# A hybrid backbone layer with hierarchical experts: router by token halves, four places for projection weights, reordered first unit

## The reference, cut to what matters

```
out_x = (sigmoid(ga) * (ya' @ w_proj_a) + sigmoid(gb) * (yb' @ w_proj_b)) @ w_out
x     = x + mx[2] * out_x
h     = rmsnorm(x, norm2_g) * (1 + mx[4]) + mx[3]
p_grp = softmax(h @ w_rg + b_rg)            # 4 groups, the best one is taken
e_sel = (h @ w_re + b_re) of that group     # 8 experts in it, the best two are taken
cw    = pg * softmax(e_sel)[top 2] / their sum
y     = sum over the 32 experts of cw[:, e] * ((silu(h @ w1[e]) * (h @ w3[e])) @ w2[e])
out   = rmsnorm(x + mx[5] * y, final_g)
```

## Time and profile before

| | us |
|---|---|
| median of 3 runs | 1008.64 (1008.11 to 1009.26) |
| the profiled execution's own time | 1011.78 |
| its span | 1010.0 |
| TensorE busy in the span | 870.7 (86%) |
| VectorE busy | 375.9 (37%) |
| ScalarE busy | 315.1 (31%) |
| moved by DMA | 284.4 MB, 282 GB/s on average |

### The profile page before, as it was taken

One profiled execution on the slowest core, in us unless ns is written; L12 is line 12 of the kernel. 1 busy time (PEld: TensorE's weight loads), 2 busy tenths in 40 slices (PEclk: granted clock), 3 DMA queues, 4 the chain that ended last, 5 costly groups with the idle time before them and its releaser, 6 DMA issues.

```text
span 1010.0 us, 13145 instructions
## 1 busy us (share of the span) xinstructions
PE 870.7 (86%) x4774; PEld 538.4 (53%) x4774; DVE 375.9 (37%) x882; ACT 315.1 (31%) x576; POOL 65.0 (6%) x109
## 2 busy tenths in 40 slices
PE   2999999999999999999998999496555746799796
PEld 1578686868686868688857433222121211343331
DVE  2357575848484848482124624100001000001101
ACT  5373737373746464640003301101010010110211
POOL 1020201111111111120000000000000000000000
PEclk9999999999999999999997999887787877899898
DMA  9956363636363635308699699999999999999993
GB/s 366 321 135 188 94 188 93 187 93 187 93 186 94 180 101 166 83 7 285 215 430 363 249 427 419 430 427 426 429 428 427 428 430 427 427 426 430 426 421 129
DMA packets 125313, 284.37 MB, mean 282 GB/s; under 512 B 6432, under 2 KB 100832, under 8 KB 111456
## 3 DMA queue, kind: packets, MB, share of 16 engines
q1 hardware_dynamic: 124656, 283.30, 74.6%
q10 hardware_dynamic: 624, 0.62, 0.2%
HBM read 282.86 MB, written 1.05 MB: 281 GB/s over the span
## 4 chain that ended last, share of the span: by engine, by line
PE 67%; DMA 25%; issue 3%; DVE 2%; ACT 1%; SPq 1%; POOL 1%; ACTq 0%; DVEq 0%; POOLq 0%
PE bank L549 37%; DMA arena<-in_w 24%; PE bank L838 11%; PE bank L847 4%; PE bank L770 3%; PE bank L857 2%; PE bank L827 2%; DMA arena<-in_c_ctx 1%; PE bank L582 1%; PE bank L637 1%; PE bank L867 1%; PE bank L654 1%; PE bank L663 1%; PE bank L618 1%; PE bank L617 1%
## 5 line engine op out<-in xcount | busy, mean ns | idle before, releaser
L549 PE MATMUL bank<-arena 128*128 128x256 f32 (+3 forms) x1792 | 401.7, 381 | 2.1 <-DVE arena L1240 1.5
L549 PEld LDWEIGHTS bank<-arena 128*128 128x128 f32 x1792 | 299.2, 191 | 86.3 <-issue 56.7
L838 PE MATMUL bank<-arena 128*32 128x512 f32 (+1 forms) x1024 | 159.2, 670 | 69.5 <-DMA arena<-in_w 69.5
L838 PEld LDWEIGHTS bank<-arena 128*32 128x32 f32 (+1 forms) x1024 | 43.9, 128 | 182.7 <-issue 110.8
L847 PE MATMUL bank<-arena 128*32 128x512 f32 (+1 forms) x512 | 80.2, 673 | 28.3 <-DMA arena<-in_w 28.3
L1564 DVE TENSOR_TENSOR arena<-arena,bank 128x512 f32<-128x512 f32 x10 | 10.3, 1030 | 235.3 <-PE bank L838 235.3
L1129 ACT ACTIVATE arena<-bank 128x512 f32<-128x512 f32 x10 | 6.0, 597 | 205.5 <-PE bank L838 205.5
L1571 DVE TENSOR_TENSOR arena<-bank,arena 128x512 f32<-128x512 f32 x20 | 13.8, 692 | 144.9 <-PE bank L847 144.9
L847 PEld LDWEIGHTS bank<-arena 128*32 128x32 f32 (+1 forms) x512 | 21.9, 129 | 79.3 <-issue 48.5
L1133 ACT ACTIVATE arena<-bank 128x256 f32<-128x256 f32 x10 | 3.8, 383 | 138.4 <-PE bank L892 138.4
L827 PE MATMUL bank<-arena 128*128 128x128 f32 x352 | 43.3, 284 | 1.7 <-DVE arena L1544 1.7
(11 more groups left out here) (304 smaller groups left out, 889.5 us busy)
## 6 DMA issues: line engine op xcount, KB each, us to landing
arena<-in_w SPq DMA_DIRECT2D x92, 2048.0 KB, 27.1
arena<-in_w_in SPq DMA_DIRECT2D x72, 512.0 KB, 7.0
arena<-in_w_mod SPq DMA_DIRECT2D x9, 2048.0 KB, 8.1
arena<-in_w SPq DMA_DIRECT2D x8, 1024.0 KB, 22.4
arena<-in_w_mod SPq DMA_DIRECT2D x1, 4096.0 KB, 17.1
arena<-in_w_proj_a SPq DMA_DIRECT2D x8, 512.0 KB, 3.8
arena<-in_w_proj_b SPq DMA_DIRECT2D x8, 512.0 KB, 5.1
arena<-in_w_out SPq DMA_DIRECT2D x2, 2048.0 KB, 9.4
```

The costliest lines, as they stand in the source:

```text
L549: i = mm(dst, w(k), rhs(k), start=k == 0, stop=k == KT - 1)
L838: i = mm(acc[w * b:w * b + w, :], xg[:, k, w * b:w * b + w], wtile(kind, b, u)[:, k, :], start=k == 0, stop=k == KT - 1)
```

## The change

It has these parts.

1. *Projection weights:* `wp` has four places instead of two; blocks 2 and 3 are asked for as soon as the last head's `og`/`ga` product is done. Then SyncE's order is: both halves of w_out, loads 0 and 1 of the experts, blocks 4 and 5, load 2, blocks 6 and 7, load 3, x and final_g, and the other loads from 4 on. Load 4 waits for block 5, load 5 for block 7. RING begins at other places so that this fits. TensorE's loop over blocks is unrolled.
2. *Modulation rows:* diagonals and `gate_rows` go, and so do `spread`, `turned`, `octet` and the matmuls of L808. TensorE turns modB once (`turn_mod`), ScalarE writes the 32 rows of 128 to a buffer in HBM and reads back gate1 and gate2, spread to all partitions, and `mod_pk`, by four DMAs on its own queue.
3. *Router by halves:* the shift term is summed on VectorE first and needs one matmul. TensorE's order is mixed: output part (1,1) is cut in pieces of 2, 4 and 2 of its eight steps, between them the logits of token half 0 and transposes. VectorE does norm and `route(t)` for half 0 while TensorE ends part (1,1), then for half 1. ScalarE makes root and xn half by half.
4. *First gather:* by token half too, with `hot` made straight from the ranks, `idle_work` matmuls whose result nobody reads between its parts, and the copies to xg shared by ScalarE and VectorE.
5. *Unit 0:* its down projection stands before the next gather; `gated(0)` stands before the four sums of the tables rk, ck; loads 10 and 11 (w2 of unit 1, in the places of unit 0's w1) come in two halves, the first when half of the w1 product is done (`m1_half`).

The core of the diff, lines of waits and views left out:

```diff
-RING = tuple(SLOT * i for i in (1, 2, 3, 4, 5, 6, 0)) + (A_T, 7 * SLOT, A_HT)
+RING = tuple(SLOT * i for i in (2, 3, 4, 5, 0, 1, 6)) + (A_T, 7 * SLOT, A_HT)
...
-        wp = [[at(2048 * b + 1024 * j, KT, P) for j in range(2)] for b in range(2)]
+        wp = [[at(2048 * b + 1024 * j, KT, P) for j in range(2)] for b in range(4)]
...
+                if n in (4, 5):
+                    sp.wait_ge(S("proj_mm1"), n - 1)
                 if n == 7:
                     sp.wait_ge(S("wo_mm"), 4)
                 if n == 8:
-                    sp.wait_ge(S("rt_mm"), 1)
+                    sp.wait_ge(S("rt_mm"), 3)
...
+                if n == 10:
+                    sp.wait_ge(S("m1_half"), 1)
+                    for i in range(2):
+                        sp.dma_start(wslot(k, i, at_u)[:, 0:2 * D], src[k][experts[i]][:, 0:2 * D]).then_inc(S("in_w2_1"), 16)
...
+            sp.wait_ge(S("ff_mm"), this(HEADS - 1))
+            proj_loads(0)
+            proj_loads(1)
+            sp.wait_ge(S("og_mm"), this(HEADS - 1))
+            proj_loads(2)
+            proj_loads(3)
+            sp.wait_ge(S("yb_out"), this(HEADS - 1))
+            sp.wait_ge(S("ya_out"), this(HEADS - 1))
+            for i in range(2):
+                sp.dma_start(wo[:, 4 * i:4 * i + 4, :], wo_v[:, 4 * i:4 * i + 4, :]).then_inc(S("wo_in"), 16)
+            sp.wait_ge(S("gb_mm"), this(HEADS - 1))
+            fetch(0)
+            fetch(1)
+            proj_loads(4)
+            proj_loads(5)
+            fetch(2)
+            proj_loads(6)
+            proj_loads(7)
+            fetch(3)
...
-                if first:
-                    gate_rows(b)
+                if first and b == 0:
+                    turn_mod()
+            def turn_mod():
+
+                pe.wait_ge(S("mod_rows"), 1)
+                pe.wait_ge(S("orms_out"), this(HEADS - 1))
+                pe.wait_ge(S("on_out"), this(HEADS - 1))
+                pe.transpose(bank[6][0:4 * KT, 0:P], modB[:], ident[:]).then_inc(S("mod_rows"), 1)
...
-            down_k(bank[2][:, 0:NG + NE], lambda k: ones[:, 0:P], lambda k: w_sh[:, k, :]).then_inc(S("gate_mm"), 1)
+            mm(bank[2][:, 0:NG + NE], ones[:, 0:P], w_sum, start=True, stop=True).then_inc(S("rt_mm"), 1)
             w_out_half(1, 0)
-            turn_x1(0)
-            w_out_half(1, 1)
+            turn_x1(0, 0)
+            turn_x1(0, 1)
+            w_out_half(1, 1, 0, 2)
             pe.wait_ge(S("rt_prep"), 2)
             pe.wait_ge(S("x1T_out"), 2)
-            logits(0)
-            turn_x1(1)
+            logits(0, 0, KT)
+            w_out_half(1, 1, 2, 6)
+            turn_x1(1, 0)
+            w_out_half(1, 1, 6, KT)
+
+            sel = rt[:, 5]
+            pe.wait_ge(S("sel_out"), 1)
+            mm(bank[7][:, 0:NE], before[:], sel[:, 0, :], start=True, stop=True).then_inc(S("rank_mm"), 1)
+            mm(bank[5][:, 0:NE], ones[:, 0:P], sel[:, 0, :], start=True, stop=False)
+            mm(bank[6][:, 0:NE], ones[:, 0:P], sel[:, 0, :], start=True, stop=False)
             pe.wait_ge(S("x1T_out"), 3)
+            logits(1, 0, 2)
+            turn_x1(1, 1)
+            logits(1, 2, 4)
             pe.wait_ge(S("x1T_out2"), 1)
+            logits(1, 4, KT)
...
+            pe.wait_ge(S("hot_first"), 1)
+            pe.wait_ge(S("xn_out"), 1)
+            gather_first(0, 0)
+            gather_first(0, 1)
+            idle_work(4)
+            pe.wait_ge(S("sel_out"), 2)
+            mm(bank[5][:, 0:NE], before[:], sel[:, 1, :], start=False, stop=True).then_inc(S("rank_mm"), 1)
+            mm(bank[6][:, 0:NE], ones[:, 0:P], sel[:, 1, :], start=False, stop=True).then_inc(S("rank_mm"), 1)
+            idle_work(1)
...
-                gather(0)
-                pe.wait_ge(S("gtc"), this(q))
-                gather(1)
+                if u != 0:
+                    gather(0)
+                    pe.wait_ge(S("gtc"), this(q))
+                    gather(1)
+                else:
+                    pe.wait_ge(S("gtc"), this(q))
...
                 down(CY, 1, u, n).then_inc(S("my"), 1)
+                if u == 0:
+                    gather(0)
+                    gather(1)
...
+            A(modT, bank[6][0:4 * KT, 0:P], ACT.Copy).then_inc(S("mod_rows"), 1)
+            act.wait_ge(S("mod_rows"), 3)
+            act.dma_start(mod_dram.rearrange("(a p) -> a p", p=P), modT).then_inc(S("mod_rows"), 16)
+            act.wait_ge(S("mod_rows"), 19)
+            act.dma_start(gate1, mod_dram[None, 0:D].to_broadcast([P, D])).then_inc(S("mod_in"), 16)
+            act.dma_start(gate2, mod_dram[None, 3 * D:4 * D].to_broadcast([P, D])).then_inc(S("mod_in"), 16)
+            act.dma_start(mod_pk, mod_dram[D:3 * D].rearrange("(j p k) -> p j k", j=2, k=KT)).then_inc(S("mod_in"), 16)
...
+            residual(0, 0)
+            residual(0, 1)
+            dve.wait_ge(S("rt_mm"), 1)
+            tt(b_rt[:], b_rt[:], bank[2][:, 0:NG + NE], ALU.add).then_inc(S("rt_prep"), 1)
+            mean_square(0)
+            residual(1, 0)
+            inverse_root(0)
+            route(0)
+            residual(1, 1)
+            ranks(0)
             dve.wait_ge(S("x1_T"), 4)
             cp(x1T[:, 4:8, P:], bank[3][:].rearrange("p (k n) -> p k n", k=4)).then_inc(S("x1T_out2"), 1)
+            mean_square(1)
+            inverse_root(1)
+            route(1)
+            ranks(1)
...
+            gated(0)
             for src_, dst in ((rank, rk), (cw[:], ck)):
                 for t in range(2):
                     link(sums(dst[:, t, FIXED:NE], order, src_[:, t, :]))
-            gated(0)
```

More of the change, by code:

```diff
@@ L135, in build @@
         aff1 = sb("aff1", 2, KT)
-        aff2 = sb("aff2", KT)
+        aff2 = modB[:, 16:24]
         ssq = sb("ssq", 4)
@@ L763, in _, with w_out_half @@
             pe.wait_ge(S("wo_in"), 32)
-            pe.wait_ge(S("gate_rows"), 2)
-            def w_out_half(t, hf):
-                for k in range(KT):
+            def w_out_half(t, hf, first=0, end=KT):
+                for k in range(first, end):
                     if (t, hf) == (0, 0) and k >= KT - 2:
@@ L801, in _ @@
             pe.wait_ge(S("x1T_out"), 3)
+            logits(1, 0, 2)
+            turn_x1(1, 1)
+            logits(1, 2, 4)
             pe.wait_ge(S("x1T_out2"), 1)
-            logits(1).then_inc(S("rt_mm"), 1)
-            pe.wait_ge(S("consts"), 6)
-            pe.wait_ge(S("rt_prep"), 3)
-            for k in range(KT):
-                i = mm(bank[6][:, 0:2 * 8], spread[:, 112 - 16 * k:240 - 16 * k], turned[:, k, :],
-                       start=k == 0, stop=k == KT - 1)
-            i.then_inc(S("rt_mm"), 1)
@@ new lines, in _, with gather_first @@
+            first_banks = [bank[4], bank[2], bank[7], bank[3]]
+            def gather_first(t, half):
+                for kt in range(4 * half, 4 * half + 4):
+                    i = mm(first_banks[kt // 2][:, P * (kt % 2):P * (kt % 2) + P], xn[:, t, P * kt:P * kt + P],
+                           hot[:, t, :], start=t == 0 and kt % 2 == 0, stop=t == 1, skip_group_check=True)
+                return i
+            pe.wait_ge(S("hot_first"), 1)
+            pe.wait_ge(S("xn_out"), 1)
+            gather_first(0, 0)
@@ L839, in up @@
                                wtile(kind, b, u)[:, k, :], start=k == 0, stop=k == KT - 1)
+                    if u == 0 and kind == "w1" and k == KT // 2 - 1:
+                        i.then_inc(S("m1_half"), 1)
                 return i
@@ L914, in _ @@
             for half in range(2):
-                gather(half)
+                gather_first(1, half).then_inc(S("mx"), 1)
             for at_u, (_, n) in enumerate(UNITS):
@@ L1121, in xg_out @@
                 i.then_inc(S("xgc"), 1)
-            for half in range(2):
-                xg_out(half, 0)
             def hidden(q, more=True):
@@ L1466, in _ @@
-            link(dve.tensor_reduce(octet[:], ident[:].rearrange("p (a b) -> p b a", b=8), AX.X, ALU.add))
-            dve.wait_ge(S("inter_mm"), this(HEADS - 1, 1))
-            for n, v in enumerate((modB[:, 8:16], aff2[:])):
-                i = tt(turned[:, :, 8 * n:8 * n + 8], octet[:].unsqueeze(1).to_broadcast([P, KT, 8]),
-                       v.unsqueeze(2).to_broadcast([P, KT, 8]), ALU.mult)
-            i.then_inc(S("rt_prep"), 1)
-            dve.wait_ge(S("gate_rows"), 2)
-            dve.wait_ge(S("xr_in"), 48)
@@ L1531, in _, with xg_first @@
[L1531 to L1537 removed]
+            rt_one, rt_two, rt_rank = rt[:, 3], rt[:, 4], rt_w[:, 2]
+            def xg_first(half):
+                dve.wait_ge(S("mod_in"), 48)
+                dve.wait_ge(S("mx"), this(0, half))
+                for k in range(2):
+                    kt = 4 * half + 2 + k
+                    i = ts(xg[:, kt, :], bank[2 + half][:, P * k:P * k + P], mod_pk[:, 1, kt:kt + 1],
+                           mod_pk[:, 0, kt:kt + 1], ALU.mult, ALU.add)
+                i.then_inc(S("xg_first"), 1)
```

320 lines of the change are left out of this document (147 added, 173 removed).

## The result

The changed kernel takes **1006.48 us** (median of 20 runs, 1004.78 to 1008.85); the kernel before, run beside it, 1009.05 us (20 runs, 1006.0 to 1011.71). The ratio is 0.9975, 95% interval 0.9967 to 0.9983: faster by 2.6 us, where 6.7 were forecast. 1006.48 lies half a microsecond outside the range of 996.5 to 1006.0.

What follows compares the result with a forecast made beforehand. The end was taken to move with TensorE's end of unit 1's down projection: 11.0 us earlier less a 4.3 us projection stall is 6.7, so 1011.8 becomes 1005.1, less 3.1 for the median: 1001.9 us, range 996.5 to 1006.0.

Steps and rivals of the forecast that it cites:

- S-Y: TensorE from first projection (S) to what follows unit 1's down projection (Y), whose end was forecast 11.0 us earlier before the stall.
- S-W: TensorE from first projection (S) to the start of w_out's product (W); 60.0 us forecast.
- Stall 4.3 us: TensorE waits for projection 4's weights, queued behind w_out, two experts and gate rows; 4.3 us lost, bounds 0 to 7.
- rival (b): TensorE's clock falls, in the projection stall or between 536 and 544; 1.5 to 3 us more, 1004.2; chance 0.20.
- W-U: TensorE from the start of w_out's product (W) through the router to unit 0's w1 (U); 41.3 us forecast.
- U-Y: TensorE from unit 0's w1 (U) to what follows unit 1's down projection (Y); 57.0 us forecast.
- costs the bare 0.6: Unit 0's down projection before the gather: waits for ScalarE's 0.60 us copy of gT and gives unit 1 nothing.
- 11.0 less 4.3: Unit 1's down projection ending 11.0 us earlier, less the 4.3 us projection stall: 6.7 us gained.
- Rival (a): No projection stall: gate rows hardly touch the stream, w_out at full rate; the whole 11.0 us gained, 997.6; chance 0.18.
- (c): Queued loads share the engines, so projection weights land late; 13.5 us lost against 11.0 won, 1011.1; chance 0.04.
- (d): The end hangs on bytes already late, not on unit 1; the gain is the stream's, 999.2; chance 0.05.
- the dip before load 20: Sign named: a small hole of 2 to 3 us in the DMA stream before expert load 20.

Runs made afterwards that it cites:

- e3: Changed kernel with six 512-wide matmuls, results unread, ahead of TensorE's wait for projection block 4; 1005.41 us.
- e4: Changed kernel with ScalarE's reads of the gate rows and mod_pk held back until block 4 is computed; 1003.62 us.
- e1: Changed kernel with SyncE's order changed after w_out: blocks 4, 5, expert load 0, block 6, load 1, block 7, loads 2, 3; 1000.13 us.
- e2: Changed kernel with projection blocks 4 to 7 all asked for ahead of expert loads 0 to 3; 1000.98 us.
- e5: e1 with unit 0's next gather put back ahead of its down projection; 997.47 us.
- e7: e1 without the five idle_work filler matmuls; 999.51 us.
- e12: The same kernel as e1, run once more; 1000.16 us.
- e9: e1 with unit 0's gather ahead of its down projection, loads 10 and 11 whole, and three more router filler matmuls; 997.49 us.
- e10: Changed kernel, SyncE's order untouched, with unit 0's gather put back ahead of its down projection; 1005.49 us.
- e11: Kernel before with five router filler matmuls: two ahead of half 1's logits, three ahead of the wait for the selection; 1007.91 us.
- e6: e1 with loads 10 and 11 whole again and without m1_half; 999.46 us.

## Why the prediction was wrong

The mechanism was right: the end moves with TensorE's end of unit 1's down projection. In all traces but one the last load lands 377.8 to 379.0 us behind it, while S-Y runs from 154.4 to 165.0. The medians follow S-Y, though not closely: median less S-Y lies between 841.9 and 844.6 in all fourteen rows of the table. The direction was right too. The sizes were not. The forecast puts Y 158.3 us behind S; it was 163.7, so 5.4 us were missing in the trace, and 4.6 in the medians. By legs, forecast against trace of the changed kernel:

- **S-W: 60.0 forecast, 63.9 measured.** The forecast step was "Stall 4.3 us". The wait was 5.3, so the sum over the queue (w_out, two experts, gate rows, block 4) was 1 us short: block 4 was in at 481.8 where I had 481.7, but this execution's S is 0.8 us earlier. The larger error is what I put beside it as rival (b) and left at nothing in the sum: the clock fell in the wait and cost 2.8 us more (30.72 us for the last four blocks, 27.89 in e3 and e4). **This is the step that failed: a wait of this length on TensorE had to be priced with the clock behind it**, and the earlier trace rows had shown that it can fall in this kernel. Wait and clock make 8.1 us of this leg; e1 gave back 8.4 of S-W and 6.3 of the time. How much of the time the clock alone was worth is less sure: its 2.8 us are plain in the traces, but the median of e3 fell by 1.1 only.
- **W-U: 41.3 forecast, 42.5 measured** (49.9 before). Routing half 1 took 3.93 us for 4.0 forecast. The 1.2 us are the small steps round it: the logits of half 1 end 35.1 us behind W for 34.4, and from the selection to w1 it is 3.4 us for 2.8. The clock stayed up in this trace, as I assumed, but fell in six of the eleven others with the new router (e1, e2, e4, e5, e7, e12), at 1.1 to 2.6 us of W-U each.
- **U-Y: 57.0 forecast, 57.4 measured** (56.3 before). I had the sign: the new order "costs the bare 0.6". I didn't draw the consequence, that this part of the change makes the kernel slower; U-Y is 1.2 us shorter in all three traces with the gather first (e5, e9, e10).

By legs the change lost 5.1, won 7.4 and lost 1.1: 1.3 us at Y, where 11.0 less 4.3 had been forecast. The medians say 2.6, with an interval of 1.7 to 3.3; that single traces differ by as much is seen in e1 and e12.

Of the rivals, (b) is what happened, in the projections and not in the router, and at its price (2.8 for 1.5 to 3); the other shortfalls came on top, so that 1006.48 stands against its 1004.2. The wait bears it out that an idle TensorE lost its clock; for the router I had read narrow work as little work, and e11 doesn't bear that out as a full account, since the clock fell there with TensorE busy without a break. Rival (a) fails on the wait, (c) on its length and on e1's order of arrival, (d) on Y-L. Of the signs that I had named, the wait at block 4 for DMA, the full clock from 530 to 560, the busy DMA engines from 454 to 505 (share 1.06) and the end of the hole at 556 were there, and so was the dip before load 20, though smaller (share 0.81 over 5 us, so about 1 us for 2 to 3). Missing from the forecast was the new hole from 525 to 543, since load 7 still waits for w_out's product. The tail, which I had as untouched, takes 16.4 us behind L in the trace before and 14.6 in this one; that was the clock of one execution (see the legs). Bytes fetched early were worth nothing (e2), and what they cost was the projection weights' place in the queue.

The rule of the Trainium skill on shared DMA engines ("DMA: Bandwidth & Descriptors", section "Issuing engines are not separate DMA queues") was the one without a row at the time. e4 now shows it: holding back ScalarE's 1.07 MB shortened the wait on SyncE's load by 2.56 us.

## What to carry to other kernels

Find the last instruction whose end a stream still waits for, and count a prefetch as worth nothing if the ring is full ahead of it. A load that an engine needs soon goes ahead of large ones that nobody needs yet: the same bytes in another order gave 6 us. A wait on TensorE that the trace shows to drop the clock costs its length and the slow stretch behind it, so it is to be priced as one term.

## What the runs showed of the hardware that I had not expected

- A DMA can hold its issuer. With 8.4 MB queued ahead, the issue of 0.5 MB in rows of 512 bytes lasted 18.59 us, 16.0 in e4, 5.0 in e1 with less ahead; the issues of experts (16 KB a partition) lasted 2.0 us at most in the changed kernel, but two in e1 lasted 4.78 and 6.55. SyncE's next load waited as long, ready or not.
- An idle stretch of 2.73 us left the granted clock at 1.0 (e4); one of 5.29 us brought it to 0.5 until 487 us, half of 2.4 GHz, and 2.8 us were lost. With fillers in the same wait it stayed at 1.0 (e3).
- ScalarE's write of 16 KB to HBM took 5.9 us to land beside the full stream, and the reads that follow 10.2, 14.6 and 15.7 us; they were needed only at 519, with the first part of w_out's product.
- In the router the clock fell in some executions and not in others of nearly the same code (gather 2.03 in e6, 3.47 in e1, 3.76 in e12). In e11 it fell although TensorE had been busy without a break since 536, from 536.6 on with matmuls of 36, 128, 288 and 16 columns.
